# Turning tiles by halves of 64 rows: a 128x128 transpose split in two in a fused two-block kernel, with two output banks taken at a time

## What is computed

```python
def reference(x, c, ctx, ...):
    x = first_block(...)      # RMS norm + modulation, projections, two mixers, merge, residual
    return second_block(...)  # 2 layers: norm, projections, 3 attentions, gate, w_out, residual

# inside first_block
oa  = gla_chunked(...)        # first mixer: 4 heads of 128, output normed per head, gated
y_a = rmsnorm(oa) * silu(ag)  # later multiplied with w_gla_out
q, k, v = conv3x3(...)        # second mixer (delta rule): causal conv of 12 tiles of 128 channels
ob  = gdn_chunked(q, k, v, ...)  # chunks of 64 tokens, 4 heads, two directions
# inside each hybrid layer
h = rms_norm(x, g_pre); z = h @ w_in
```

## Time and profile before

| what | value |
|---|---|
| median of 3 runs | 1321.48 us (1321.43 to 1322.52) |
| profiled execution | 1320.69 us, span 1318.9 us |
| PE busy | 1273.5 us (97%) |
| DVE, ACT, POOL busy | 694.4, 413.4, 395.4 us |
| mean granted PE clock | 0.995 |
| HBM read | 92.89 MB |

### The profile page before, as it was taken

The page is one execution under the profiler, slowest core; times in us unless marked ns, Lnnn a source line. Parts: engine busy times, 40 slices in busy tenths (PEclk is TensorE's granted clock), DMA queues, the critical chain, the costliest instruction groups (busy, mean ns, idle before and its releaser), DMA issues.

```text
span 1318.9 us, 24624 instructions
## 1 busy us (share of the span) xinstructions
PE 1273.5 (97%) x9971; PEld 778.4 (59%) x9971; DVE 694.4 (53%) x1422; ACT 413.4 (31%) x898; POOL 395.4 (30%) x470
## 2 busy tenths in 40 slices
PE   5999999999999999999999999998999999999997
PEld 3454555555656667687445885455645786446653
DVE  4366667847334444574473563247636374237735
ACT  4244213263432322101024002346613102236721
POOL 0100000212324543172432320138631250128731
PEclk9999999999999999999999999999999999999999
DMA  9710112101220100043326315110004415100001
GB/s 316 277 64 6 60 65 80 46 18 65 88 108 3 67 2 3 2 141 115 142 77 136 96 32 192 64 53 1 2 16 98 134 33 191 64 1 2 1 1 64
DMA packets 71535, 96.59 MB, mean 73 GB/s; under 512 B 27639, under 2 KB 35247, under 8 KB 71422
## 3 DMA queue, kind: packets, MB, share of 16 engines
q1 hardware_dynamic: 71050, 94.76, 21.6%
q10 hardware_dynamic: 372, 0.27, 0.1%
HBM read 92.89 MB, written 2.13 MB: 72 GB/s over the span
## 4 chain that ended last, share of the span: by engine, by line
PE 85%; DVE 5%; SPq 3%; POOL 3%; ACT 2%; issue 1%; DMA 1%; POOLq 0%; DVEq 0%; ACTq 0%
PE PS L147 81%; PE PS L2822 2%; POOL AR L3109 1%; SPq L187 1%; DVE AR L2928 1%; POOL AR L2045 1%; DMA bias_rows<-AR 1%; SPq L308 1%; ACT AR L3050 0%; SPq L312 0%; SPq L304 0%; SPq L309 0%; DVE AR L2098 0%; DVE AR L2915 0%; POOL AR L3107 0%
## 5 line engine op out<-in xcount | busy, mean ns | idle before, releaser
L147 PE MATMUL PS<-AR 64*64 64x64 f32 (+13 forms) x9334 | 1200.7, 326 | 19.8 <-ACT AR L3060 5.1
L147 PEld LDWEIGHTS PS<-AR 64*64 64x64 f32 (+5 forms) x9334 | 708.2, 152 | 482.0 <-issue 386.8
L3050 ACT ACTIVATE AR<-AR 128x257 f32<-128x257 f32 (+5 forms) x160 | 84.9, 531 | 98.3 <-DVE AR L2928 88.8
L2928 DVE CUSTOM_DVE_ANT_0 AR<-PS,AR 128x257 f32<-128x257 f32 (+5 forms) x160 | 72.2, 451 | 61.2 <-PE PS L147 43.8
L412 POOL TENSOR_TENSOR AR<-AR 128x1 f32<-128x1 f32 (+4 forms) x26 | 21.9, 841 | 257.9 <-DVE AR L407 211.1
L1189 DVE SCALAR_TENSOR_TENSOR AR<-AR 128x441 f32<-128x441 f32 (+2 forms) x96 | 78.6, 818 | 15.7 <-ACT AR L1146 12.0
L1607 DVE TENSOR_TENSOR AR<-PS,AR 128x256 f32<-128x256 f32 x60 | 25.5, 424 | 86.9 <-PE PS L147 83.7
L3109 POOL TENSOR_SCALAR AR<-AR 128x257 f32<-128x257 f32 (+5 forms) x96 | 53.4, 556 | 58.8 <-DVE AR L2934 51.3
L3107 POOL TENSOR_SCALAR AR<-AR 128x128 f32<-128x128 f32 (+3 forms) x64 | 38.9, 609 | 63.3 <-DVE AR L2934 58.3
L2045 POOL TENSOR_TENSOR AR<-AR 128x512 f32<-128x512 f32 x36 | 47.4, 1318 | 28.1 <-DMA AR<-in_w_o 25.1
L2822 PE MATMUL PS<-AR 128*128 128x128 f32 x352 | 50.9, 282 | 4.9 <-DVE AR L2915 3.2
(11 more groups left out here) (264 smaller groups left out, 952.6 us busy)
## 6 DMA issues: line engine op xcount, KB each, us to landing
AR<-in_w_in SPq DMA_DIRECT2D x16, 2048.0 KB, 9.0
AR<-in_w_mod SPq DMA_DIRECT2D x6, 2048.0 KB, 12.7
AR<-in_w_out SPq DMA_DIRECT2D x4, 2048.0 KB, 12.7
AR<-in_x SPq DMA_DIRECT2D x8, 512.0 KB, 5.0
AR<-in_w_in SPq DMA_DIRECT2D x4, 1024.0 KB, 7.5
AR<-in_w_o SPq DMA_DIRECT2D x2, 2048.0 KB, 7.8
AR<-in_w_in SPq DMA_DIRECT2D x2, 1664.0 KB, 8.7
AR<-in_w_in SPq DMA_DIRECT2D x12, 256.0 KB, 4.2
```

The lines of the kernel that those rows point to most:

```text
L147: return t.matmul(o, l, r, start=s, stop=p, skip_group_check=True)
L2928: v.do.tensor_tensor_reduce(PB[j % NJP][e][:, 0:nk], ps["s", l, j, e][:, 0:nk], bias_for(qb, kind, 2 * a + e, nk), 1.0, 3e38, ALU.add, ALU ...
L3050: a_.do.activation(P, P, ACT.Exp, bias=mn[:, j % NJS, e:e + 1], scale=-1.0, accum_out=su[:, j % NJS, e:e + 1]).then_inc(sa, na("p", l, j, e))
```

## The change

Each 128x128 transpose becomes two, over partitions 0 to 63 and 64 to 127, which write 64 columns each. The two halves r = 0 and r = 1 go to two different banks and are issued in turn. Each activation that empties a bank then writes chunks of 64 columns. Both banks of a group are taken before its first transpose, and one semaphore count stands at the end of the group in place of one for each bank. In ya the pairs of banks are named by number (0 and 1, then 2 and 3), and `ps.k += 4` counts the ring on as four takes would.

```diff
     def gated_t(t, sq, name):
-        for h in range(4):
-            p = ps.take(t, "yT", name, h)
-            for a in range(4):
-                x = t.go.transpose(p[:, 128 * a:128 * a + 128], sv4[:, a, h, :], ident)
-            x.then_inc(st, nt("yT", name, h))
+        for hp in range(2):
+            p = ps.take_two(t, "yT", name, hp, bank=2 * hp)
+            for h in (2 * hp, 2 * hp + 1):
+                for a in range(4):
+                    for r in range(2):
+                        c = 512 * r + 256 * (h % 2) + 64 * a
+                        x = t.go.transpose(p[:, c:c + 64], sv4[64 * r:64 * r + 64, a, h, :], ident[64 * r:64 * r + 64, 64 * r:64 * r + 64])
+            x.then_inc(st, nt("yT", name, hp))
+        ps.k += 4
     def gated_a(a, yT, onorm, name):
-        for h in range(4):
-            a.wait_ge(st, nt["yT", name, h])
-            a.do.activation(yT[:, h, :], ps["yT", name, h][:, :], ACT.Copy, bias=0.0, scale=onorm).then_inc(sa, na("y", name))
-            ps.empty(sa, na, "yT", name, h)
+        for hp in range(2):
+            a.wait_ge(st, nt["yT", name, hp])
+            for r in range(2):
+                dst = yT[:, 2 * hp:2 * hp + 2, :].rearrange("p h (a r x) -> p h a r x", r=2, x=64)[:, :, :, r, :]
+                src = ps.two("yT", name, hp)[:, 512 * r:512 * r + 512].rearrange("p (h a x) -> p h a x", h=2, a=4)
+                a.do.activation(dst, src, ACT.Copy, bias=0.0, scale=onorm).then_inc(sa, na("y", name))
+            ps.empty(sa, na, "yT", name, hp)
@@ delta_t
-            for name, src in (("kN", KT), ("vN", VT)):
-                p = ps.take(t, name, a)
+            p = [ps.take(t, "kvN", a, r) for r in range(2)]
+            for i, src in enumerate((KT, VT)):
                 for h1 in range(2):
                     for c in range(2):
-                        at = 256 * a + 128 * c
-                        x = t.go.transpose(p[:, blk_of(2 * h1, c, 128)], src[:, h1, at:at + 128], ident)
-                x.then_inc(st, nt(name, a))
+                        at, o = 256 * a + 128 * c, 256 * i + 64 * (2 * h1 + c)
+                        for r in range(2):
+                            x = t.go.transpose(p[r][:, o:o + 64], src[64 * r:64 * r + 64, h1, at:at + 128],
+                                               ident[64 * r:64 * r + 64, 64 * r:64 * r + 64])
+            x.then_inc(st, nt("kvN", a))
@@ delta_a
-            for name, dst in (("kN", KNd), ("vN", VK)):
-                a_.wait_ge(st, nt[name, a])
-                a_.do.activation(dst[:, a, :], ps[name, a][:, :], ACT.Copy, bias=0.0, scale=1.0).then_inc(sa, na(name, a))
-                ps.empty(sa, na, name, a)
+            a_.wait_ge(st, nt["kvN", a])
+            for r in range(2):
+                k_, v_ = (x[:, a, :].rearrange("p (b r x) -> p b r x", r=2, x=64)[:, :, r, :] for x in (KNd, VK))
+                both = bass.AP(tensor=k_.tensor, offset=k_.offset, ap=[list(k_.ap[0]), [v_.offset - k_.offset, 2], list(k_.ap[1]), list(k_.ap[2])])
+                a_.do.activation(both, ps["kvN", a, r][:, :].rearrange("p (i b x) -> p i b x", i=2, b=4), ACT.Copy, bias=0.0, scale=1.0).then_inc(sa, na())
+                ps.empty(sa, na, "kvN", a, r)
@@ turned_row, turned_row_a
-        for i in range(2):
-            p = ps.take(t, "h2", l, a, i)
-            for m in range(4):
-                x = t.go.transpose(p[:, 128 * m:128 * m + 128], xns[l][:, a, 512 * i + 128 * m:512 * i + 128 * m + 128], ident)
-            x.then_inc(st, nt("h2", l, a, i))
+        p = [ps.take(t, "h2", l, a, r) for r in range(2)]
+        for m in range(8):
+            for r in range(2):
+                x = t.go.transpose(p[r][:, 64 * m:64 * m + 64], xns[l][64 * r:64 * r + 64, a, 128 * m:128 * m + 128],
+                                   ident[64 * r:64 * r + 64, 64 * r:64 * r + 64])
+        x.then_inc(st, nt("h2", l, a))
```

More of the change, by code:

```diff
@@ L1721, in delta_a @@
         for a in TILES:
-            for name, dst in (("kN", KNd), ("vN", VK)):
-                a_.wait_ge(st, nt[name, a])
-                a_.do.activation(dst[:, a, :], ps[name, a][:, :], ACT.Copy, bias=0.0, scale=1.0).then_inc(sa, na(name, a))
-                ps.empty(sa, na, name, a)
+            a_.wait_ge(st, nt["kvN", a])
[4 more added lines that the diff above has]
+                ps.empty(sa, na, "kvN", a, r)
+            na.mark("kN", a)
+            na.mark("vN", a)
             if a == 1:
@@ L1803, in delta_g @@
             lower(n, 0)
-        g.wait_ge(st, nt["vN", TILES[-1]])
+        g.wait_ge(st, nt["kvN", TILES[-1]])
         for n in range(2):
@@ L2152, in turned_row @@
         t.wait_ge(sv, nv["xrow", l, a])
-        for i in range(2):
-            p = ps.take(t, "h2", l, a, i)
-            for m in range(4):
-                x = t.go.transpose(p[:, 128 * m:128 * m + 128], xns[l][:, a, 512 * i + 128 * m:512 * i + 128 * m + 128], ident)
-            x.then_inc(st, nt("h2", l, a, i))
+        p = [ps.take(t, "h2", l, a, r) for r in range(2)]
[4 more added lines that the diff above has]
+        x.then_inc(st, nt("h2", l, a))
     def turned_row_a(a_, l, a):
-        for i in range(2):
-            a_.wait_ge(st, nt["h2", l, a, i])
-            a_.do.activation(hT2[:, 4 * i:4 * i + 4, 128 * a:128 * a + 128], ps["h2", l, a, i][:, :].rearrange("p (m n) -> p m n", m=4),
+        a_.wait_ge(st, nt["h2", l, a])
+        for r in range(2):
+            c = 128 * a + 64 * r
+            a_.do.activation(hT2[:, :, c:c + 64], ps["h2", l, a, r][:, :].rearrange("p (m n) -> p m n", m=8),
                              ACT.Copy, bias=0.0, scale=1.0).then_inc(sa, na("h2", l, a))
-            ps.empty(sa, na, "h2", l, a, i)
+            ps.empty(sa, na, "h2", l, a, r)
     def wo_t(t):
@@ L2418, in two_s @@
         wukv = I["mla_w_ukv_2"][l].rearrange("p (h c) -> p h c", h=4)
-        s.wait_ge(st, nt["h2", l, 3, 1])
+        s.wait_ge(st, nt["h2", l, 3])
         for k in range(2):
@@ L2710, in two_g @@
         ng.mark("at", f"layer{l}")
-        g.wait_ge(st, nt["h2", l, 3, 1])
+        g.wait_ge(st, nt["h2", l, 3])
         for z in (SKb[:, :, 0:1], KC, HS4, Pc, RC[0][:, :, 31:32], RC[1][:, :, 31:32]):
```

## The result

The changed kernel takes 1325.37 us (median of 7 runs, 1323.40 to 1327.58); the kernel before took 1321.55 us on the same chip (7 runs, 1321.20 to 1322.52). The ratio is 1.0028, 95% interval [1.0016, 1.0039]: slower by 0.28%, 3.8 us. The prediction said 1323.9 with a range to 1325.4, so the time lies 0.03 us inside the range's upper end, and on the side to which 0.35 was given and not 0.62.

A forecast was written before the change was run, and what follows sets the result against it. PE was taken to bound the kernel (busy 97% of the span, 85% of the chain). +2.3 - 0.8 - 1.0 + 0.4 = +0.9, with the clock's +1.5 +2.4 us, on median 1321.48 gave 1323.9 us; range 1321.3 to 1325.4.

The forecast's parts named there:

- ya, +2.3: First mixer's output: conv 2 must wait for bank 3, emptied only after the last of ScalarE's four activations; +2.3 us.
- The bank is not waited for: Rival at conv 2: count mistaken or evictions end in time; sum -1.9 us, 1319.6, not slower; chance 0.07.
- evictions dearer through their chunks: Rival: each eviction 0.1 us dearer in ya, the layers and delta; 1325.3; chance 0.10.
- The clock, +1.5: PE idles 2.8 us before conv 2, the clock halves, and conv's dense products pay 1.2 to 1.7 us; 1.5 taken.
- Rival 1: The wait on bank 3 comes without a fall of the clock: +0.9 us, 1322.4; chance 0.30.
- Price of a pair and of a change of shape: Transposes: 0.06 us per pair of halves in turn; 0.15 us per shape change, two per group in ya and layers.
- The halves don't overlap: Rival on all half transposes: a pair costs 0.12 us, 1326.8 to 1328.3, clearly slower; chance 0.04.
- Layers, -0.6: Both layers: row tiles 0 and 1 save 0.49 us each layer (-1.0); row tiles 2 and 3 cost 0.19 each (+0.4).
- delta, -0.8: Delta rule: tiles five and six save 0.39 us each in transposes, so turn(0) starts 0.8 us earlier.
- rival 4: Other waits: each eviction 0.1 us dearer through its chunks, in ya, the layers and delta; 1325.3; chance 0.10.

The follow-up runs named there:

- the first mixer's part alone: The kernel before with only the first mixer's functions (gated_t, gated_a) taken from the changed kernel; 1325.18 us, ratio 1.0029.

## Why the prediction was right, and where it failed

**ya, +2.3: right, 2.19 measured.** The mechanism was the one named: conv 2 behind bank 3, the bank behind the last of four evictions. The prediction put conv 2 at 3.98 us after the first transpose; it was 3.83, because the evictions came to 2.93 us and not 3.03 and began 0.05 us sooner. *The bank is not waited for* is excluded by the same row, and *evictions dearer through their chunks* too: they are a little cheaper (2.57 us for four in the layers, 2.67 to 2.68 where the rows are turned whole).

**The clock, +1.5: right, 1.69 measured** in the changed kernel's profile and 2.9 (5.13 - 2.19) in that of the first mixer's part alone. The low end of 1.2 assumed that part of the fall passes in the wait; in the changed kernel it began 0.5 us after the wait's end and fell wholly on dense products. Rival 1, no fall, got 0.30, and neither profile shows it: both in which PE stood idle in this wait have a fall there, and none of those in which it worked through the wait or did not wait. Two profiles don't tell how often a run goes without.

**Price of a pair and of a change of shape: right together.** 0.063 measured for a pair in a stream, against 0.06. From first transpose to next product it is 1.15 and not 1.26, but 0.10 comes back behind it (ya's 0.59 shrink to 0.49 over the stretch; the group (1, 4) reaches row tile 2 after 713.34 - 698.63 = 14.71 us where row tile 2 is turned whole, where it took 14.61 before). In the changed kernel it takes 14.81, another 0.10 with the change ahead of row tile 2's halves. The net for ya is the -0.48 forecast. *The halves don't overlap* was priced at 0.12 a pair; the experiment gives 0.09 for halves that really are not in turn. By the rule of the Trainium skill ("TensorE: Matmul & The Clock Gate", LDWEIGHTS), that a weight load's time goes by its columns, a half's load of 128 columns should have taken as long as a whole one's. As the prediction priced it that is 0.218 a pair, and the 32 transposes in 1.15 us exclude it here, as do the 1.56 us with the halves not in turn. The rule on the change of mode held: the Trainium skill ("TensorEngine Tiling (Array Packing)", Key Properties) has tiles of one mode run in parallel, and the halves in turn do, by 0.026 us a pair; a change of the division isn't free, as the 0.10 shows.

**Layers, -0.6: half right.** Row tiles 0 and 1 save the 0.49 forecast up to small(2), row tiles 2 and 3 cost 0.17 (0.19 forecast). Over a whole layer 0.24 and 0.20 arrive, 0.16 in all less than forecast; of these the 0.20 is the firmer, since layer 0 scatters by 0.37 us between kernels that leave it alone.

**delta, -0.8: the step that failed.** Up to turn(0) it was right. Timeline of the changed kernel, against the earlier trace rows:

```profile
343.14 0.72 PE L1433 MATMUL PS<-AR 64*128 64x64 f32 x16
...
351.79 1.10 PE L147 MATMUL PS<-AR 128*64 128x128 f32 x16 [0.84 <-ACT AR L1735]
352.82 0.72 PE L1433 MATMUL PS<-AR 64*128 64x64 f32 x16
353.47 1.10 PE L147 MATMUL PS<-AR 128*64 128x128 f32 x16
...
355.14 1.15 PE L147 MATMUL PS<-AR 64*64 64x64 f32 x32
```

Tiles five and six take 0.65 us each for their transposes, and turn(0) starts at 355.14, 12.00 us after the first transpose at 343.14, where it was 351.56 - 338.73 = 12.83.

The prediction took the gain as arrived there, since it found no wait behind that would take it back. What it put at nothing without a reason is the supply of instructions: the change moves the instruction stream itself. The kernel before shows no such stop in its rounds, the changed kernel loses 1.60 us at 375 us, and 128 instructions put at the start give it back. No row of the kernel before priced this; but its rows told that 64x64 products go by in bursts, and a change that adds 128 instructions to TensorE ahead of such bursts should have had a rival for it, and a bound. With this term the sum is 2.4 + 1.6 = 4.0 us, against 3.8 between the medians.

So the forecast came near by its two large terms, and the one that was missing turned a doubtful "no difference" into a loss that can be measured. That the time still lies inside the range is luck: the room above the forecast was meant for rival 4, dearer evictions, which did not come, and the stop, which nobody had in mind, filled it to the last 0.03 us.

## What to carry to other kernels

When a unit of work is made larger (two banks and four evictions where one was), ask first who takes the bank next: an allocation that "keeps its old alignment" may hand the very next product the bank that is now emptied last. A wait in front of a dense stream costs more than its length, since the clock may fall behind it; if it can't be removed, work that fits into it pays (1.7 us here), and work that is longer than the wait costs more than it saves. And compare the trace behind the edit as well: a gain up to one point can be lost to a stop that no semaphore explains, and such a stop can be moved by a few dozen instructions placed where the engine waits anyway.

## What the runs showed of the hardware

- TensorE can run out of instructions. A packet of its instruction queue carries about 256 and takes 0.9 to 1.3 us; in bursts of 64x64 products PE uses about 100 a microsecond. The seven stops seen were 0.17 to 1.34 us of "issue", and each ended 2.39 to 2.50 us after the start of a packet. Six stood behind exactly 2504 matmuls, in four different places of the burst. Shifted by 80 instructions the stream had its stop 78 us later, shifted by 128 it had none.
- The clock fell to 1.2 GHz after a stretch in which PE was busy 0.81 of 3.41 us, and in another kernel after one with 1.75 of 3.41 and stayed low through one with 2.48, all in front of or within products that fill PE wholly. With the same wait filled it did not fall there. The fall in front of dense products cost 1.69 us for 3.41 us at half clock; one in layer 1 cost nothing that the stretch shows.
- Two half transposes in turn cost 0.063 us, one after the other 0.09, a whole one 0.109. A change between half tiles and whole ones shows 0.10 us of its price only behind the first product that follows.
